# Input projections of the second block as three fp32r products of split operands, with the score matrix packed as a triangle

## The reference, cut to what matters

```python
u = rmsnorm(h, norm1_w[l])
proj = jnp.einsum('bsd,de->bse', u, w_in[l])      # 512x1024 by 1024x3584
qa, ka, va = proj[..., :a], proj[..., a:2 * a], proj[..., 2 * a:3 * a]
qb, fb, ib, gb = ...                              # four more of 512 columns
ya = dilated_attention_group(qa, ka, va)          # 8 heads of 64
yb = hgrn2_group(qb, fb, ib, gb, lb_table[l], hgrn_norm_w[l])
h = h + jnp.einsum('bse,ed->bsd', jnp.concatenate([ya, yb], axis=-1), w_out[l])
...
```

## Time and profile before

| | us |
|---|---|
| median of 3 runs | 2225.14 (2224.36 to 2225.99) |
| the profiled execution, whole time | 2224.99 |
| its span in the trace | 2222.9 |
| stage from the first matmul of tile 0 to the end of tile 19 | 1482.1 to 1656.9 |
| value steps and attention loop | 1656.9 to about 1790 |

### The profile page before, as it was taken

The page is one execution under the profiler, slowest core; times in us unless marked ns, Lnnn a source line. Parts: engine busy times, 40 slices in busy tenths (PEclk is TensorE's granted clock), DMA queues, the critical chain, the costliest instruction groups (busy, mean ns, idle before and its releaser), DMA issues.

```text
span 2222.9 us, 26223 instructions
## 1 busy us (share of the span) xinstructions
PE 2153.6 (97%) x8888; PEld 1436.8 (65%) x8888; DVE 1488.8 (67%) x1474; ACT 1075.6 (48%) x1006; POOL 236.5 (11%) x239
## 2 busy tenths in 40 slices
PE   8999999999999999999999999959999999999998
PEld 3445447777777777777777777624654557888886
DVE  3953459999999999999999999843642323333333
ACT  1010147777777777777777777620003423222222
POOL 0003301211111121111112111100000000000000
PEclk9998989999999999999999999969999999999999
DMA  6123379999999999999999999822131011222220
GB/s 259 57 83 118 120 290 344 379 373 385 368 387 371 384 377 375 379 375 383 373 384 376 377 379 373 325 68 76 48 105 38 38 38 68 99 104 99 100 90 38
DMA packets 77757, 522.38 MB, mean 235 GB/s; under 512 B 10208, under 2 KB 10736, under 8 KB 21392
## 3 DMA queue, kind: packets, MB, share of 16 engines
q1 hardware_dynamic: 65088, 483.68, 56.0%
q0 software_dynamic: 9168, 31.01, 5.5%
q10 hardware_dynamic: 3456, 7.06, 1.0%
HBM read 500.72 MB, written 18.99 MB: 234 GB/s over the span
## 4 chain that ended last, share of the span: by engine, by line
PE 92%; DVE 5%; ACT 1%; DMA 1%; issue 0%; SPq 0%; DVEq 0%; ACTq 0%; POOLq 0%
PE bank L1021 21%; PE bank L1023 21%; PE bank L1022 21%; PE bank L887 8%; PE bank L1133 6%; DVE room L1338 3%; PE bank L1176 3%; PE bank L1234 2%; PE bank L1037 1%; PE bank L1148 1%; PE bank L993 1%; PE bank L1029 1%; PE bank L1206 1%; PE bank L1225 1%; PE bank L896 1%; PE bank L1188 1%
## 5 line engine op out<-in xcount | busy, mean ns | idle before, releaser
L1485 DVE TENSOR_TENSOR ring_r<-ring,room_r 128x2048 fp32r<-128x2048 f32 x384 | 873.5, 2289 | 89.6 <-ACT room_r L637 86.7
L637 ACT ACTIVATE room_r<-ring 128x2048 fp32r<-128x2048 f32 x384 | 735.5, 1916 | 189.1 <-PE bank L1023 183.4
L1021 PE MATMUL bank<-room_r 128*96 128x512 f32 x1536 | 606.7, 395 | 3.5 <-DVE room_r L1517 1.9
L1023 PE MATMUL bank<-room_r 128*96 128x512 f32 x1536 | 602.7, 392 | 0.0
L1022 PE MATMUL bank<-ring_r,room_r 128*96 128x512 f32 x1536 | 602.5, 392 | 0.0
L1021 PEld LDWEIGHTS bank<-room_r 128*96 128x96 f32 x1536 | 248.4, 162 | 105.9 <-DVE ring_r L1485 4.4
L1023 PEld LDWEIGHTS bank<-room_r 128*96 128x96 f32 x1536 | 248.2, 162 | 106.2
L1022 PEld LDWEIGHTS bank<-ring_r,room_r 128*96 128x96 f32 x1536 | 248.5, 162 | 101.4
L1133 PE MATMUL bank<-room,ring 128*128 128x512 f32 x320 | 140.4, 596 | 0.0
L1021 PE MATMUL bank<-room_r,ring_r 128*128 128x512 f32 x352 | 137.0, 389 | 0.9 <-DVE room_r L1736 0.9
L1023 PE MATMUL bank<-room_r,ring_r 128*128 128x512 f32 x352 | 136.9, 389 | 0.0
(11 more groups left out here) (249 smaller groups left out, 2189.5 us busy)
## 6 DMA issues: line engine op xcount, KB each, us to landing
ring<-in_wmoe SPq DMA_DIRECT2D x384, 1024.0 KB, 11.7
ring<-in_wf SPq DMA_DIRECT2D x33, 1024.0 KB, 4.8
ring<-in_wp SPq DMA_DIRECT2D x9, 2048.0 KB, 7.8
ring<-in_wd SPq DMA_DIRECT2D x7, 2048.0 KB, 8.6
ring<-in_wd SPq DMA_DIRECT2D x3, 1024.0 KB, 8.3
room<-in_xT SPq DMA_DIRECT2D x2, 1024.0 KB, 8.6
room<-in_xtok ACTq DMA_DIRECT2D x1, 2048.0 KB, 7.7
h_rows<-room POOLq DMA_DIRECT2D x4, 512.0 KB, 3.0
```

What stands on the lines that cost most here:

```text
L637: act.activation(w_hi[s_ % PAIRS], raw_w[ORDER[s_]], ACT.Copy)\
L1021: pe.matmul(out, x_hi, w_hi, start=start, stop=False, skip_group_check=True)
L1023: return pe.matmul(out, x_lo, w_hi, start=False, stop=stop, skip_group_check=True)
L1485: dve.tensor_tensor(w_lo[i], raw_w[i], w_hi[s_ % PAIRS].bitcast(F32), ALU.subtract)\
```

## The change

Every matmul of `p_tile` and `vt_step` becomes a `product` of three fp32r matmuls. For that:

- `uT` becomes `uT_hi` (ACT, all eight banks) and `uT_lo` (DVE, all eight, each after ACT's high part).
- A weight load is half as large (1 MB, two tiles; for the values four steps of k) and lands in the upper half of a slot. There are 14 halves. ACT makes the high part in the lower half of the slot (`half_hi`), DVE makes the low part in place (`half_lo`). Halves 0 to 2 are split before `combine`. The others are split between the tiles, the levels and the attention iterations, at places written out in the code.
- The order of value steps changes for groups 4 and 5, which take turns by half (`VT_ORDER`).
- `AT` keeps only the blocks on and above the diagonal (5120 columns, not 8192). Six of the eight tiles of `uT_lo` live in what this frees. The clearing of `AT` shrinks with it, and the copies of level 9 become eight of 256 columns.
- The two 2 MB loads of `w_out` get a tensor of their own and wait for value tiles 4 and 8.

```diff
+            def half_hi(h):
+                half_in(act, h)
+                act.activation(p_hi[h % RING2], p_raw[h % RING2], ACT.Copy).then_inc(s["fhi_done"], 1)
+            for h in range(RING2):
+                half_hi(h)
...
-            for k in range(0, KT, 2):
+            for k in range(KT):
                 act.wait_ge(s["unT_ready"], k + 1)
-                act.activation(uT[:, k, :], bank[k][:, :], ACT.Copy, ...).then_inc(s["uT_done_a"], 1)
+                act.activation(uT_hi[:, k, :], bank[k][:, :], ACT.Copy, ...).then_inc(s["uT_done_a"], 1)
...
+                if j >= 2 and j % 2 == 0:
+                    half_hi(j // 2 + 2)
...
             def p_tile(j):
-                w = chunk2(pe, j // 4).rearrange("p (k c) -> p k c", k=KT)
+                pe.wait_ge(s["flo_done"], j // 2 + 1)
...
-                        pe.wait_ge(s["uT_done_v" if k % 2 else "uT_done_a"], k // 2 + 1)
-                    ins = pe.matmul(bank[j % 2][:, :], w[:, k, c:c + P], uT[:, k, :], ...)
+                        pe.wait_ge(s["uT_done_v"], k + 1)
+                    ins = product(bank[j % 2][:, :], hi[:, k, c:c + P], lo[:, k, c:c + P], uT_hi[:, k, :], uT_lo[k],
+                                  k == 0, k == KT - 1)
...
+            def half_lo(h):
+                dve.wait_ge(s["fhi_done"], h + 1)
+                dve.tensor_tensor(p_lo[h % RING2], p_raw[h % RING2], p_hi[h % RING2].bitcast(F32), ALU.subtract)\
+                   .then_inc(s["flo_done"], 1)
...
                 if n >= 5:
                     rotate(n - 5)
+                if n % 2:
+                    half_lo(6 + n // 2)
+            half_lo(11)
             for m in range(5, 8):
                 rotate(m)
...
             for u in range(AHEAD):
                 masked(u)
+            half_lo(12)
...
+                if u == LAST_HALF:
+                    half_lo(13)
```

More of the change, by code:

```diff
@@ L77 @@
 VT_STEPS = [3 * KT, 3 * KT + 4, 4 * KT] + [4 * KT + (3 * n + 1) // 2 for n in range(1, 22)] + [8 * KT] * 9
-VT_DONE = [next(u for u in range(HEADS * TT) if VT_STEPS[u + 1] >= KT * (g + 1)) for g in range(3, 8)]
+VT_ORDER = [(g, k) for g in range(4) for k in range(KT)] \
+    + [(g, k) for half in range(2) for g in (4, 5) for k in range(4 * half, 4 * half + 4)] \
+    + [(g, k) for g in (6, 7) for k in range(KT)]
+VT_DONE = [next(u for u in range(HEADS * TT) if VT_STEPS[u + 1] > VT_ORDER.index((g, KT - 1))) for g in range(3, 8)]
 O_AT = [24, 26, 28, 30]
@@ L90 @@
 RING2 = 3
-POST = 9
+HALVES = 14
+LAST_HALF = 4
+AT_ROW = [q * S - P * (q * (q - 1) // 2) for q in range(TT + 1)]
+AT_HEAD = AT_ROW[TT]
 FFN_HALVES = FFN_T + FFN_T // 2
@@ L250, in build @@
         att_s = sb("att_s", [P, 3 * AHEAD])
-        uT = hT
+        uT_hi = vr(0, KT * S).rearrange("p (k t) -> p k t", k=KT)
+        uT_lo = [ring_at(4 * CH + HG_HEADS * AT_HEAD + n * S, S, ring_r) for n in range(6)] \
+            + [ring_at(3 * CH + n * S, S, ring_r) for n in (0, 7)]
         qkT = v(4096, 8 * S).rearrange("p (m t) -> p m t", m=8)
@@ L286, in build @@
         u2T_lo = vr(20480, KT * S).rearrange("p (k t) -> p k t", k=KT)
+        p_hi = [ring_at(n * CH, HW, ring_r) for n in range(RING2)]
+        p_raw = [ring_at(n * CH + HW, HW) for n in range(RING2)]
+        p_lo = [ring_at(n * CH + HW, HW, ring_r) for n in range(RING2)]
         fraw_w = [ring_at(n * HW, HW) for n in (0, 1, 6)]
@@ L324, in build @@
                      ("mix_ready", 7), ("mix_ready", 8), ("pleg_ready", 7), ("pleg_ready", 8), ("plep_ready", 8)])
[L326 to L328 removed]
+        post_used = [("p_ready", 2 * (h + 1)) for h in range(10)] + [("vt_ready", 4)]
+        assert len(pre_used) == PRE and len(post_used) == HALVES - RING2
         def chunk_cols(n):
@@ L351, in counted, with at_cols, half_in, out_rows @@
             return 3 if edge and s in (1, 2) else 1
[L353 to L357, removed]
+        def at_cols(h, q, t, n):
+            at = h * AT_HEAD + AT_ROW[q] + t - q * P
+            return AT[:, at:at + n]
+        def half_in(eng, h):
+            q = h % RING2
+            eng.wait_ge(chunk_in[q], 16 * (PRE_SLOT.count(q) + h // RING2 + 1))
+        def out_rows(eng, n):
+            q = 2 - n
+            eng.wait_ge(chunk_in[q], 16 * (PRE_SLOT.count(q) + len(range(q, HALVES, RING2)) + 1))
+            return slot(q).rearrange("p (k c) -> p k c", k=KT)
         def xt_bank(b, q):
@@ L415, in _ @@
                     block_loads(b, False)
-            for n in range(POST):
+            for n in range(HALVES):
                 if n < RING2:
@@ L432, in _ @@
                         sp.dma_start(acc[:, i, :], sum_dram[i * P:(i + 1) * P, :]).then_inc(sum_in[i], 16)
+            for n in range(2):
+                sp.wait_ge(s["vt_ready"], 4 + 4 * n)
+                sp.dma_start(slot(2 - n), a["wo"][n]).then_inc(chunk_in[2 - n], 16)
             for f in range(FFN_HALVES):
@@ L1175, in vt_step @@
                 i = g % 4
-                ins = pe.matmul(bank[6 + g % 2][:, :], uT[:, k, i * P:(i + 1) * P], w[:, k, :], start=(k == 0), stop=(k == KT - 1))
+                ins = product(bank[6 + g % 2][:, :], uT_hi[:, k, i * P:(i + 1) * P], uT_lo[k][:, i * P:(i + 1) * P], hi, lo,
+                              k == 0, k == KT - 1)
                 if k == KT - 1:
```

62 lines of the change are left out of this document (38 added, 24 removed).

## The result

The changed kernel takes 2198.23 us (2197.31 to 2198.82), the kernel before took 2225.56 (2224.36 to 2226.31) beside it: a ratio of 0.988 (95% interval 0.9867 to 0.9893). That is 27.3 us less where 34.6 were forecast, inside the range of 2184 to 2202 and where the first rival stood (2194 to 2203).

The account below looks back on a forecast made before the run. PE was taken as the bound, with DVE ending later in the levels; savings 12.2 (entry, tiles 0 to 7) + 5.9 (levels) + 4.6 (tiles 17 to 19) + 12.2 (value steps) - 0.3 = 34.6 us, giving 2190.4; range 2184 to 2202.

Parts of the forecast that it names:

- the first rival: Hand-overs between ACT, DVE and PE late at more places: 4 to 12 us lost, 2194 to 2203; chance 0.20.
- the three low parts that it named (5, 11 and 13): Weight halves in tiles, value steps and attention loop: DVE finishes each just before PE wants it, covers 0.2 to 0.5 us.
- Splitting halves 0 to 2 (nothing): Ahead of `combine`: splits end at about 1456.5, before the sums at 1458.25, cover 1.8 us, so no cost.
- The price of a product: In tiles and value steps: three matmuls take 0.667 us, at most 0.674, against 0.858 for a plain matmul.
- farther apart than 0.225 us: Sign that the forecast is wrong: product records on PE spaced by more than this.
- Weight loads hidden: In every product: three weight loads of 0.188 us each run beside the matmuls and add no time.
- the fourth rival: Weight loads not hidden in products: 1.23 us each, 83 us slower than before, 2308; chance 0.01.
- Entry at half the clock: Start of tile 0: PE at 1.2 GHz until about 1484.4, doing 1.5 steps of k; entry and tiles 0 to 7 save 12.2.
- Levels: Levels 0 to 9: PE waits for DVE's update and copies, so nine tiles save 5.9 us and not 13.8.
- Value steps: 64 value steps before and in the attention loop: save 12.2 us, less 0.3 for a late last rotation.
- The second rival: Slow-clock stretch near 1440 absent (1.5 to 2 us), fewer level waits (some 4 us): 2184 to 2187; chance 0.09.
- Packed `AT`: Score matrix: nothing changes on the path; clearing 3/8 shorter, level 9's copies some 0.3 us longer, not waited for.

Follow-up runs that it names:

- best version: Changed kernel with both expert loops ended at 32 blocks, low parts 8 and 9 moved, and four wide copies per level instead of sixteen: 2187.27 us, ratio 0.9828.
- GpSimd run: Changed kernel with both expert loops ended at 32 blocks, low parts 8 and 9 moved, and the hK update made by GpSimd instead of DVE: 2199.98 us, ratio 0.9883.
- two products: The best version with the low-activations by high-weights product left out of the value steps: 2178.22 us in a single run.

## Why the prediction was right, and where it was not

- **The sum** was 34.6 us, the medians give 27.3. The forecast's own range (2187 to 2194) missed, and the wider range of 2184 to 2202 held. The time fell where the first rival stood (late hand-overs), and that is luck in part: PE waited for none of the three low parts that it named (5, 11 and 13), and no rival spoke of the loops. In the traced executions 1.6 us of the gain are also a slow stretch in the exit that went, which has nothing to do with the change (see the value steps below).
- **"Splitting halves 0 to 2 (nothing)" is the step that failed**, by 6.7 us. It took ACT to be free when its last work ended. ACT was free 8.1 us later, and DVE later than that. The working (1448.3 + 5.8 + 2.3 = 1456.5) is right once the loops end with their work: 1458.2, 1.2 us ahead of the sums. The prediction did say that if its cover were gone, the excess would be paid in full, and it was. Four runs show it: ending ACT's loop gives 1.9, splitting ahead of the empty iterations 3.7, ending both loops 6.9, and in the kernel before that gives nothing.
- **The price of a product was 0.667, and is 0.680.** The term was taken from 90 records in 20 us. In a stretch a record is counted that only reaches into it, so it holds some 88 starts. PE's timeline has the distance itself, in the kernel after, in tile 0 (the start is what counts, not the 0.39):

```profile
1493.66 0.39 PE L1065 MATMUL bank<-room_r,ring_r 128*128 128x512 f32 x1
1493.88 0.39 PE L1063 MATMUL bank<-room_r,ring_r 128*128 128x512 f32 x1
1494.11 0.39 PE L1064 MATMUL bank<-ring_r 128*128 128x512 f32 x1
...
1502.72 0.39 PE L1063 MATMUL bank<-room_r,ring_r 128*128 128x512 f32 x1
```

  The last row is 40 starts behind the first. The distance is 9.06 / 40 = 0.227 us, so 5.44 for a tile, and a saving of 0.178 and not 0.191 a product. For tiles 0 to 7 that is 0.8 of the 1.0 missing, for tiles 17 to 19 it is 0.3, for the 64 value steps 0.8. The mark "farther apart than 0.225 us" in the prediction's last part was met.
- **Weight loads hidden: right.** A load of 0.19 us stands beside each matmul of 0.227 us. The sentence of the Trainium skill (TensorE: Matmul & The Clock Gate, Part 3, "The mechanism") that speaks for the fourth rival does not hold for these full loads, and the 83 us it would have cost did not come.
- **Entry at half the clock: right.** The granted clock is 0.50 and then 0.98, and the slow stretch ended in the second step of k. Stretches of the kernel after (columns as above):

```profile
1489.40:1491.40 2.00, 1.97 (x5) 1.61 (x6) 2.00 (x4) 2.00 (x5) 0.00 (x0) 0.50 0.03 8
1491.40:1493.40 2.00, 2.00 (x10) 1.68 (x9) 2.00 (x4) 1.98 (x3) 0.00 (x0) 0.98 0.00 0
```

- **Levels: right**, 5.8 for 5.9, and by its mechanism. The steps from level to level were forecast at 9.32, 10.57, 10.02, 9.72, 9.57, 9.52 and 9.97; measured were 9.48, 10.66, 10.13, 9.87, 9.73, 9.67 and 9.67. Six are 0.1 to 0.16 too small. The last is too large, because it charged low part 8. Two waits were too large as well: 1.36 us ahead of level 2 for 1.6, and 0.56 ahead of level 9 for 1.3.
- **Value steps: 1.3 us too good.** From the scores to `w_out` it is 9.5 for 9.2, but 1.6 of it is no merit of the change: before, PE's clock fell to 0.50 in the exit (1773.91, 4.54 us for 24), and after it did not (1749.06, 2.92 us). The wait ahead was 1.54 us in both. It also fell in the best version (4.54), and it did not fall in the kernel before with merged copies (2.92), so it belongs to neither kernel. The second rival had priced such a stretch at 1.5 to 2 us, at another place. Of the 1.3 us the price explains 0.6. The rest stays open: four iterations take 12.36 where the price of a product and the rows of before (13.32) make 12.25.
- **Packed `AT`: right**, nothing.

## What to carry to other kernels

When work is put behind a loop, ask when each engine leaves the loop, not when its last useful instruction ends: an "issue" gap ahead of the first instruction behind it is the price, and it hides as long as that instruction waits for something else. When a stage's main engine gets cheaper, the helper's chain is the new bound, and savings on it that were worth next to nothing then count, as long as the main engine waits (here 0.7 us per level: 0.2 us from level 0 to level 9 before, 4.9 after). The cost of a stream is the distance of two starts in the timeline; a count of records in a stretch includes those that only reach into it.

## What the runs showed of the hardware that I had not expected

- An iteration of a loop whose condition fails, so that nothing in it is executed, takes some 0.39 us on ACT (8.12 / 21) and 0.56 to 0.62 on DVE (11.71 and 12.92 / 21). These are estimates that give the whole gap to the 21 iterations. Why DVE's two gaps differ stays open.
- A DVE product of 1.2 us takes 2.9 to 3.9 beside one of GpSimd, and ends 1.08 us after it.
- Sixteen predicated copies of 128 columns take 3.25 us and four of 512 take 2.57. By these two, twelve copies fewer save 0.7 us and the 2048 columns take the rest (an estimate: the mask is also read in another form), so most of the time goes by columns and not by instructions.
- Waits of PE of 2.92 us (GpSimd run, level 2) and 2.19 us (two products, scores) were followed by half the clock, and one of 1.96 (GpSimd run, level 3) was not. The same wait can do either: 1.92 us at 1440 was followed by half the clock in the kernel after (0.57 over the 2 us from 1440) and by 1.00 in the run in which only ACT's loop ends, and 1.54 us in the exit by 0.50 in the kernel before and by 1.00 in the one after. So these runs don't tell from the length of a wait alone whether the clock falls.
